# Rows of the split activations at other byte offsets, a halved opening that ends with the second tile alone, and column sums placed between products

## The reference, cut to what matters

```python
def swiglu(h, w1, w2):
    a, b = jnp.split(h @ w1, 2, axis=-1)
    return (jax.nn.silu(a) * b) @ w2

h = h + 0.5 * ml[2] * swiglu(modulate(h, norm_g[l, 0], ml[0], ml[1]), ffn_w1[l, 0], ffn_w2[l, 0])   # FFN, D_FF = 2816
...
y_l, y_c = ab_mixer(...)   # layer 0: input projection, retention heads and an S5 scan with a GLU, output projection
y_l, y_c = na_mixer(...)   # layer 1: k, q, v projections, neighbourhood attention, output projection
...
h = h + 0.5 * ml[8] * swiglu(modulate(h, norm_g[l, 2], ml[6], ml[7]), ffn_w1[l, 1], ffn_w2[l, 1])
```

## Time and profile before

| | |
|---|---|
| median of three runs | 1868.72 us (1867.93 to 1872.14) |
| the profiled execution, its own time | 1870.24 us |
| its span | 1868.4 us |
| TensorE busy | 1795.8 us (96%) |
| TensorE's weight loads | 1529.7 us (82%) |
| DVE busy | 1194.8 us (64%) |
| ACT busy | 726.6 us (39%) |
| POOL busy | 61.9 us (3%) |
| mean granted TensorE clock | 0.982 of 2.4 GHz |
| chain that ended last | TensorE 84%, DVE 8%, ACT 5%, issue 2%, DMA 1% |
| read from HBM | 255.79 MB, 137 GB/s over the span |

### The profile page before, as it was taken

How to read it: one execution, slowest core, us unless ns; L and a number is a source line. 1 busy time by engine, 2 the same in 40 slices (tenths; PEclk the granted TensorE clock), 3 DMA queues, 4 the chain that set the end, 5 groups by cost and what they waited for, 6 DMA issues and landing times.

```text
span 1868.4 us, 25748 instructions
## 1 busy us (share of the span) xinstructions
PE 1795.8 (96%) x9970; PEld 1529.7 (82%) x9970; DVE 1194.8 (64%) x1890; ACT 726.6 (39%) x1027; POOL 61.9 (3%) x41
## 2 busy tenths in 40 slices
PE   7999999998988899999999999999999999989998
PEld 5788888887787588888888888888888898689997
DVE  4677677777999745776677367766333434855554
ACT  4422222336888734231222242212222333744343
POOL 0000000020000010000000200000002000010001
PEclk8999999999999899999999999999999999989999
DMA  8454455331110123544553335444213342034543
GB/s 328 182 204 156 169 193 194 113 125 60 54 35 35 46 90 113 210 161 154 196 208 125 115 136 194 154 158 175 106 65 115 124 169 68 2 136 174 186 171 122
DMA packets 40440, 257.81 MB, mean 138 GB/s; under 512 B 4752, under 2 KB 6032, under 8 KB 15536
## 3 DMA queue, kind: packets, MB, share of 16 engines
q1 hardware_dynamic: 40368, 256.86, 38.0%
HBM read 255.79 MB, written 1.05 MB: 137 GB/s over the span
## 4 chain that ended last, share of the span: by engine, by line
PE 84%; DVE 8%; ACT 5%; issue 2%; DMA 1%; POOL 0%; DVEq 0%; SPq 0%; ACTq 0%; POOLq 0%
PE ps_all L1797 26%; PE ps_all L1801 25%; PE ps_all L1798 25%; DVE w_lo L1047 2%; ACT w_hi L565 2%; PE ps_all L1793 1%; PE banks L2355 1%; DVE sq_acc L1527 1%; PE banks L2169 1%; PE ps_all L2332 0%; PE banks L1949 0%; DVE normed L1536 0%; PE banks L2332 0%; PE ps_all L1987 0%; DVE scaled L1518 0%
## 5 line engine op out<-in xcount | busy, mean ns | idle before, releaser
L1797 PE MATMUL ps_all<-a_hi,w_lo 128*128 128x512 f32 (+1 forms) x1832 | 655.1, 358 | 17.4 <-DVE w_lo L1047 8.6
L1801 PE MATMUL ps_all<-a_lo,w_hi 128*128 128x512 f32 (+1 forms) x1832 | 650.1, 355 | 0.1
L1798 PE MATMUL ps_all<-a_hi,w_hi 128*128 128x512 f32 (+1 forms) x1832 | 650.1, 355 | 0.0
L1047 DVE TENSOR_TENSOR w_lo<-w_raw,w_hi 128x2048 fp32r<-128x2048 f32 (+2 forms) x179 | 365.2, 2040 | 161.2 <-ACT w_hi L565 161.0
L565 ACT ACTIVATE w_hi<-w_raw 128x2048 fp32r<-128x2048 f32 (+2 forms) x179 | 306.0, 1709 | 332.7 <-PE ps_all L1801 316.2
L1797 PEld LDWEIGHTS ps_all<-a_hi,w_lo 128*128 128x128 f32 x1832 | 348.9, 190 | 69.1 <-DVE w_lo L1047 10.7
L1801 PEld LDWEIGHTS ps_all<-a_lo,w_hi 128*128 128x128 f32 x1832 | 348.9, 190 | 48.4 <-DVE a_lo L1201 0.3
L1798 PEld LDWEIGHTS ps_all<-a_hi,w_hi 128*128 128x128 f32 x1832 | 348.9, 190 | 47.1 <-issue 0.2
L1059 DVE SCALAR_TENSOR_TENSOR mod_junk<-mod_raw,cond 128x1024 bf16<-128x1024 f32 x256 | 302.8, 1221 | 7.4 <-ACT cond L593 5.4
L1797 PE MATMUL ps_all<-g_hi,w_lo 128*128 128x512 f32 (+1 forms) x734 | 264.4, 360 | 2.1 <-DVE w_lo L1047 2.1
L1801 PE MATMUL ps_all<-g_lo,w_hi 128*128 128x512 f32 (+1 forms) x734 | 263.3, 359 | 0.0
(11 more groups left out here) (280 smaller groups left out, 1528.6 us busy)
## 6 DMA issues: line engine op xcount, KB each, us to landing
w_raw<-in_tiles SPq DMA_DIRECT2D x118, 1024.0 KB, 4.8
mod_raw<-in_w_mod SPq DMA_DIRECT2D x64, 1024.0 KB, 4.8
w_raw<-in_tiles SPq DMA_DIRECT2D x32, 768.0 KB, 4.1
w_raw<-in_tiles SPq DMA_DIRECT2D x32, 640.0 KB, 3.8
start_w<-in_w_start SPq DMA_DIRECT2D x8, 1024.0 KB, 19.9
bias<-in_na_bias SPq DMA_DIRECT2D x2, 1536.0 KB, 9.0
h<-in_h SPq DMA_DIRECT2D x4, 512.0 KB, 5.7
cond<-in_cond SPq DMA_DIRECT2D x2, 1024.0 KB, 18.2
```

The costliest lines, as they stand in the source:

```text
L1047: nc.vector.tensor_tensor(w_lo[:, slot, 0:size], w_raw[:, slot, 0:size], w_hi[:, slot, 0:size].bitcast(F32), ALU.subtract).then_inc(lo_rea ...
L1797: pe.matmul(dst, w[1], x[0], start=start, stop=False)
L1798: pe.matmul(dst, w[0], x[0], start=False, stop=False)
L1801: return pe.matmul(dst, w[0], x[1], start=False, stop=stop_)
```

## The change

- A tensor `rows_gap` of 64 bytes a partition is declared behind `kint`, ahead of `g_hi` and of all that lies over the FFN's tensors: each of them starts 64 bytes later. `g` rows of 512 tokens then start at 1088 of 2048, their latent halves (closings) at 64.
- `LAST_AT` = columns 112 to 367 of a row, in place of 256 to 511, holds the 256 latent tokens of na_out's input (`a`) and of ffn3's `a` and `g` rows. The former start at 1024 of 2048, the latter at 1536. PSUM, `gated` and `h` keep their places.
- `halved_opening`: its last eight units are (0, 4..7), then (1, 4..7), in place of a mixed order that ended (0, 7), (1, 6), (1, 7). `opening`: (0, 7) is followed by six units of slot 1, not four, and (0, 2) comes before (1, 0).
- `mixer0`: ret_in's first weights are split before `us` is copied from tile 0 (ACT), and ahead of DVE's last of the eight copies.
- `close`: the column sums of the latent half, and those of the second-last square, are put between products of the latent half; `part(range(1), 1)` and the like say which products.

```diff
@@ -229,6 +229,7 @@
...
         kint = sbuf("kint", [P, 32], mybir.dt.int32)
+        sbuf("rows_gap", [P, 16])
 
@@ -340,6 +341,8 @@
...
         FFN_T0 = (0, 0, 0, NCTX)
+        LAST_AT = slice(112, 112 + NLAT)
+        FFN_AT = [slice(t0, T) for t0 in FFN_T0[:3]] + [LAST_AT]
 
@@ -575,7 +578,7 @@
...
                     act.wait_ge(ps_free[slot], BASE[segment] // 2 + it + 1)
-                    g = g_hi[:, bass.ds(2 * it + slot, 1), t0:T].rearrange("p a t -> p (a t)")
+                    g = g_hi[:, bass.ds(2 * it + slot, 1), FFN_AT[int(segment[3])]].rearrange("p a t -> p (a t)")
                     nc.scalar.activation(g, gated[:, slot, t0:T], ACT.Copy).then_inc(g_hi_ready, 1)
@@ -710,10 +713,8 @@
...
                     act.wait_ge(scaled_ready, KT * PART_BASE[k_norm] + k + 1)
-                    for half, b, e in halves(t0):
-                        ins = nc.scalar.activation(a_hi[:, k, b:e], ahead[k % 4][:, b:e], ACT.Identity,
-                                                   bias=modv[:, col(k_norm, 0) + k, half:half + 1])
-                    ins.then_inc(a_hi_ready, 1)
+                    nc.scalar.activation(a_hi[:, k, LAST_AT], ahead[k % 4][:, NCTX:T], ACT.Identity,
+                                         bias=modv[:, col(k_norm, 0) + k, 1:2]).then_inc(a_hi_ready, 1)
 
@@ -779,8 +780,8 @@
...
                 for j in range(2):
-                    if j:
-                        split_hi(BASE["s5_in"] + j + 1, 2048, 1 - j)
+                    if j == 0:
+                        split_hi(BASE["ret_in"], 2048, 0)
                     act.wait_ge(pe_done, BASE["s5_in"] + j + 1)
@@ -1003,7 +1004,7 @@
...
                     nc.scalar.activation(
-                        a_hi[:, tile, NCTX:T].rearrange("p (r c) -> p r c", c=GRID_W),
+                        a_hi[:, tile, LAST_AT].rearrange("p (r c) -> p r c", c=GRID_W),
                         bank[tile % 2][:, 0:NLAT].rearrange("p (r c) -> p r c", c=GRID_W)[:, :, ::-1],
@@ -1088,7 +1089,7 @@
...
                     dve.wait_ge(g_hi_ready, g_base(segment) + j + 1)
-                    hi, lo = [x[:, bass.ds(j, 1), t0:T].rearrange("p a t -> p (a t)") for x in (g_hi, g_lo)]
+                    hi, lo = [x[:, bass.ds(j, 1), FFN_AT[int(segment[3])]].rearrange("p a t -> p (a t)") for x in (g_hi, g_lo)]
                     nc.vector.tensor_tensor(lo, gated[:, slot, t0:T], hi.bitcast(F32), ALU.subtract).then_inc(g_split, 1)
@@ -1265,11 +1266,9 @@
...
                     dve.wait_ge(a_hi_ready, KT * PART_BASE[k_norm] + k + 1)
-                    for half, b, e in halves(t0):
-                        ins = nc.vector.scalar_tensor_tensor(a_lo[:, k, b:e], ahead[k % 4][:, b:e],
-                                                             modv[:, col(k_norm, 0) + k, half:half + 1],
-                                                             a_hi[:, k, b:e].bitcast(F32), ALU.add, ALU.subtract)
-                    ins.then_inc(a_ready, 1)
+                    nc.vector.scalar_tensor_tensor(a_lo[:, k, LAST_AT], ahead[k % 4][:, NCTX:T],
+                                                   modv[:, col(k_norm, 0) + k, 1:2],
+                                                   a_hi[:, k, LAST_AT].bitcast(F32), ALU.add, ALU.subtract).then_inc(a_ready, 1)
                     if k < KT - 2:
@@ -1458,12 +1457,12 @@
...
                 for j in range(2):
-                    if j:
-                        split_lo(BASE["s5_in"] + j + 1, 2048, 1 - j)
                     dve.wait_ge(pe_done, BASE["s5_in"] + j + 1)
...
                             if q == 3 and s == 3:
+                                if j == 0:
+                                    split_lo(BASE["ret_in"], 2048, 0)
                                 dve.wait_ge(S["us_act"], j + 1)
@@ -1707,9 +1706,9 @@
...
                     nc.vector.tensor_tensor(
-                        a_lo[:, tile, NCTX:T].rearrange("p (r c) -> p r c", c=GRID_W),
+                        a_lo[:, tile, LAST_AT].rearrange("p (r c) -> p r c", c=GRID_W),
                         bank[tile % 2][:, 0:NLAT].rearrange("p (r c) -> p r c", c=GRID_W)[:, :, ::-1],
-                        a_hi[:, tile, NCTX:T].bitcast(F32).rearrange("p (r c) -> p r c", c=GRID_W),
+                        a_hi[:, tile, LAST_AT].bitcast(F32).rearrange("p (r c) -> p r c", c=GRID_W),
                         ALU.subtract).then_inc(N["mix"], 1)
@@ -1811,7 +1810,8 @@
...
                                 mm = three(ps[slot][:, m, t0:T], [x[:, k, m] for x in w],
-                                           (a_hi[:, k, t0:T], a_lo[:, k, t0:T]), k == 0, k == KT - 1)
+                                           (a_hi[:, k, FFN_AT[int(segment[3])]], a_lo[:, k, FFN_AT[int(segment[3])]]),
+                                           k == 0, k == KT - 1)
                         mm.then_inc(pe_done, 1)
@@ -1836,7 +1836,7 @@
...
                         mm = three(ps[slot][:, 0, t0:T], [x[:, k] for x in w],
-                                   (g_hi[:, k, t0:T], g_lo[:, k, t0:T]), k == 0, k == K - 1)
+                                   (g_hi[:, k, FFN_AT[f]], g_lo[:, k, FFN_AT[f]]), k == 0, k == K - 1)
                     mm.then_inc(pe_done, 1)
@@ -1867,20 +1867,23 @@
...
                 half_sums(sq_acc, 0, 0)
-                half_sums(sq_acc, 0, 1)
+                part(range(1), 1)
                 if first == KT - 1:
...
                     half_sums(sq[:, 0], 1, 0)
-                    half_sums(sq[:, 0], 1, 1).then_inc(sq_summed, 1)
-                else:
-                    part(range(1), 1)
+                    part(range(1, 2), 1)
                 pe.wait_ge(sq_part, LAST_SQUARES[k_norm])
...
                 mm.then_inc(half_summed, 1)
-                part(range(0 if first == KT - 1 else 1, 4), 1)
+                part(range(2 if first == KT - 1 else 1, 4), 1)
+                half_sums(sq_acc, 0, 1)
+                part(range(4, 5), 1)
+                if first == KT - 1:
+                    half_sums(sq[:, 0], 1, 1).then_inc(sq_summed, 1)
+                part(range(5, 6), 1)
                 spread_half(k_norm, 0)
-                part(range(4, K), 1).then_inc(pe_done, 1)
+                part(range(6, K), 1).then_inc(pe_done, 1)
 
@@ -1930,7 +1933,7 @@
...
                         unit(slot, k, NCTX, T, 1)
-                for slot, k in ((0, 4), (0, 5), (1, 4), (0, 6), (1, 5), (0, 7), (1, 6), (1, 7)):
+                for slot, k in ((0, 4), (0, 5), (0, 6), (0, 7), (1, 4), (1, 5), (1, 6), (1, 7)):
                     if (slot, k) == (1, 4):
@@ -2025,10 +2028,10 @@
...
 
-                segment, t0 = AFTER_NORM[k_norm], FFN_T0[int(AFTER_NORM[k_norm][3])] if "ffn" in AFTER_NORM[k_norm] else 0
+                segment, t0 = AFTER_NORM[k_norm], NCTX
                 n = BASE[segment]
-                order = [(0, 0), (0, 1), (1, 0), (0, 2), (1, 1), (0, 3), (1, 2), (0, 4), (1, 3), (0, 5), (0, 6), (0, 7),
-                         (1, 4), (1, 5), (1, 6), (1, 7)]
+                order = [(0, 0), (0, 1), (0, 2), (1, 0), (0, 3), (1, 1), (0, 4), (0, 5), (0, 6), (0, 7),
+                         (1, 2), (1, 3), (1, 4), (1, 5), (1, 6), (1, 7)]
                 for slot, k in order:
@@ -2040,7 +2043,7 @@
...
                         mm = three(ps[slot][:, m, t0:T], [x[:, k, m] for x in w],
-                                   (a_hi[:, k, t0:T], a_lo[:, k, t0:T]), k == 0, k == KT - 1, lo)
+                                   (a_hi[:, k, LAST_AT], a_lo[:, k, LAST_AT]), k == 0, k == KT - 1, lo)
                     if k == KT - 1:
@@ -2282,7 +2285,7 @@
...
 
-            def pair_tile(segment, j, K, at, before=None, t0=0, lat=False):
+            def pair_tile(segment, j, K, at, before=None, t0=0, rows=None):
 
@@ -2293,7 +2296,8 @@
...
                         mm = three(ps[slot][:, m, t0:T], [x[:, k, m] for x in w],
-                                   (a_hi[:, at + k, t0:T], a_lo[:, at + k, t0:T]), k == 0, k == K - 1)
+                                   (a_hi[:, at + k, rows or slice(t0, T)], a_lo[:, at + k, rows or slice(t0, T)]),
+                                   k == 0, k == K - 1)
                 mm.then_inc(pe_done, 1)
@@ -2368,7 +2372,7 @@
...
                 for j in range(4):
-                    pair_tile("na_out", j, 8, 0, lambda k: pe.wait_ge(N["mix"], k + 1) if j == 0 else None, NCTX)
+                    pair_tile("na_out", j, 8, 0, lambda k: pe.wait_ge(N["mix"], k + 1) if j == 0 else None, NCTX, LAST_AT)
 
```

## The result

The changed kernel takes 1839.19 us (median of four runs, 1838.46 to 1840.89) against 1870.23 for the kernel before (median of four); the ratio is 0.983, 95% interval 0.9819 to 0.9842. That is 31.0 us faster; 1836 was forecast. Timed once more beside two other kernels, it took 1839.03 against 1870.73. Of the 3.2 us between forecast and result, 1.5 are from the time of the kernel before: 1836 was counted from the median of three runs, 1868.72, and the fourth made it 1870.23. The profiled execution has 1839.42 us, a span of 1837.6 and a mean granted clock of 0.987 (before: 1870.24, 1868.4 and 0.982).

What follows compares the result with a forecast made beforehand. Outside the mixers TensorE's step between products and its idle times bound the kernel. Rows 10.0 - 0.8 + 1.3 + 2.9, openings 7.6 + 4.1 + 1.9, clock 1.7 + 1.7 + 1.4, sums 1.3: 33.1 off 1868.72, 1836 us; range 1828 to 1850.

Steps and rivals of the forecast that it cites:

- Part 1: Rows moved by bytes: 512-column products from `g` fall from 233.3 to 226.7 ns, 10.0 us; further terms -0.8, +1.3, +2.9.
- the 0.8: Loss in the three closings, whose 180 products from `g` go to the bad start: 1.2 us, partly hidden under DVE's work.
- the bound of 3.5: Loss in us if ffn3's 528 narrow `g` products, moved to byte 1536, ran slower there; no change was taken.
- The ring in ffn3: End of tile, Silu, gating, g_hi, w_hi, w_lo, tile j+2 limits the up pass: half of 0.32 per tile kept, 2.9 us.
- The rival of 7.0 us: ffn3's weights ring gives way and its up pass keeps all of 7.0 us: 1832; chance 0.05.
- Part 2: Openings end with the second tile alone, removing or shortening TensorE's idle times: 7.6 (ffn1, ffn2, na_k) + 4.1 (s5_in) + 1.9 (ffn3).
- a sign named for being wrong: Idle times turning up within tile 0 of an opening, before L1801, for `a_lo`, would show the prediction wrong.
- The clock: Half-clock stretches behind idle times at s5_in, ffn2 and ffn3 vanish with the idle times: 1.7 + 1.7 + 1.4 us.
- rival 2: Clock still falls in closings and after short idle times that stay: 9.1 us less gain, 1845; chance 0.12.
- the retention stage shifts as a whole: ret_in's rows, evacuation and scan start from s5_in's resumed product, so the first mixer keeps its gain of 4.1 us.
- waits for POOL before and after: 0: First mixer's closing (ab_out) waits for POOL either way, so moving its column sums changes nothing: 0.
- Part 3: Column sums between products keep the clock up in three closings; the openings give back 0.45 each, 1.3 us.

Runs made afterwards that it cites:

- orders alone: The changed kernel without the 64-byte gap and with `LAST_AT` back at the old columns, so only the new opening, copy and column-sum orders; 1854.66 us, ratio 0.9906.
- rows alone: The kernel before with only the 64-byte gap, `LAST_AT` and its uses, orders as they were; 1856.62 us, ratio 0.992.
- v3: The changed kernel with both the edit of v1 and the edit of v2; 1832.09 us, ratio 0.9789.
- v1: The changed kernel, but in ffn3 w_hi and w_lo of tile j+2 are made ahead of g_hi and g_lo of tile j; 1834.14 us, ratio 0.981.
- Old sums: The changed kernel with `close` as it was before, column sums back in their old places; 1840.47 us, ratio 0.9837.
- v2: The changed kernel with 1/rms spread ahead of the second-last square's latent sums in FFN closings, two rows earlier in the first mixer's; 1835.96 us, ratio 0.9815.
- v4: v3 with the `a` rows of na_out and ffn3 back at byte 64 of 512, `g` rows left at 1536; 1837.82 us.

## Why the prediction was right, point by point

The forecast was 33.1 us, and the two traces differ by 30.8. By stretch, the terms of the sum put where they belong, and measured:

| | forecast | measured |
|---|---|---|
| three down0 (3 x 288 x 6.67 ns) | 5.8 | 5.7 |
| ffn0's closing to ffn1.up0 | 9.8 | 6.9 |
| ffn1.down1 to ffn2.up0 | 5.7 | 6.0 |
| ffn2.down1, second mixer, ffn3.up0 | 10.4 | 10.4 |
| ffn3.up1 | 1.5 | 1.4 |
| start, ffn3's down passes and end | 0 | 0.3 |

(The up1 passes of ffn0 to ffn2 give the 0.1 that is left.)

- *Part 1, `g` at 64.* Right: 226.7 ns in all 498 triples; the tiles of the down1 passes give 1.39 between *orders alone* and after, 210 x 6.67 ns. The closings' products did go to 120, but the 0.8 does not show: the closings of *orders alone* are not shorter by it. In the first half of a closing 30 products cost 0.2 more, but behind it TensorE waits for the last square (a step of 0.50 in *orders alone*, of 0.32 after, both in ffn1's closing), which takes it up. ffn3's `g` rows at 1536 behave as at 1024: the bound of 3.5 did not come in. The ground given, start modulo 512, was too coarse: the period is 256.
- *na_out.* Its 192 products took 23.01 us before and 21.77 after, 1.24 against 1.3. In *rows alone* and in v3 they took 22.6, at 117.8.
- *The ring in ffn3.* Right: 10 tiles of up1 came 0.14 nearer, forecast 0.15. That the weights' ring bound them is what v1 and v3 show together: with it away no wait is left in the pass. The rival of 7.0 us needs more than the ring: with the ring away a pass gave 0.5 in v1 and 2.6 in v3, by the step that TensorE happened to take.
- *Part 2.* Idle times are gone at ffn1, ffn2 and na_k, and 0.56 and 0.65 are left at s5_in and ffn3, forecast 0.6. ret_in's first tile starts 6.93 earlier where s5_in's second ended 2.79 earlier: 4.14 of 4.1. ffn3's (0, 2) waits 0.85 for `a_lo`, not 0.2. With this and the 0.20 and 0.60 in the other openings, a sign named for being wrong came true in small: idle times for `a_lo` inside an opening.
- *The clock.* Six stretches at half clock gone, as forecast; rival 2 did not happen in the FFNs. *Old sums* shows the price of a fall in a closing: 1.54.
- *The step that failed* is that the first mixer keeps all: "the retention stage shifts as a whole", and for its closing "waits for POOL before and after: 0". 2.9 us are missing there. Up to 0.3 more than forecast was gained before (7.67 by the product at 440.80, counted from the start of ffn0.down1, which itself comes 0.77 earlier; 7.4 was forecast); 3.2 were then lost in three places. First, with the clock up the product that stood at 440.80 comes 8.44 earlier, but `qk` (ACT's timeline, before and after) only 7.57: ACT had waited 2.19 for TensorE there and now works without a pause from the second tile's copies on. 0.9 lost.

```profile
450.21 1.02 ACT L798 ACTIVATE qk<-ps_all 128x1024 f32<-128x1024 f32 x1 [2.19 <-PE ps_all L1801]
```

```profile
442.64 1.02 ACT L799 ACTIVATE qk<-ps_all 128x1024 f32<-128x1024 f32 x1
```

  Second, the mixer's closing spread 1.4 later, and ffn1's opening waits 0.60 for `a_lo`: the closing's first sum comes 5.83 earlier than before and ffn1.down0 7.62 earlier, so closing and opening gave 1.8 of the 2.4 forecast; 0.6 lost. v2 won 0.8 back. Third, the extra stretch at 633.4 took 1.7: up to it DVE's rows are 7.6 earlier than before, behind it 5.9. It is in both traces of the changed kernel, in *orders alone*, *old sums*, v1 and v4, but not in v2 and v3, whose mixer has the same code there; neither the kernel before nor *rows alone* has it. What makes it come is open.
- *Part 3.* 1.3 forecast. Its terms were right in kind, but one was left out. Where a fall is spared, 1.54 - 0.9 = 0.6 is left, near the 0.45 of the forecast; where there would have been none, 0.9 is lost, and that had been put at 0. With falls in six of nine closings that makes 0.1 a closing (my estimate), 0.4 in place of 1.3. v2 has the gain without the cost in the FFN closings. Half w_lo is still last before product (1, 0), as forecast; at ffn2's opening it ends at 1075.04, and the product starts at 1075.10 (DVE's and TensorE's timeline):

```profile
1073.82 1.22 DVE L1226 TENSOR_TENSOR w_lo<-w_raw,w_hi 128x1024 fp32r<-128x1024 f32 x1
```

```profile
1075.10 0.39 PE L1796 MATMUL ps_all<-a_hi,w_lo 128*128 128x256 f32 x1
```

## What to carry to other kernels

Before moving work about, measure the distance of starts of like products from each source: a fixed surplus that follows the byte where a row starts can be won by a gap between tensors, here one of 64 bytes. When a closing is rearranged to keep TensorE's clock up, put what the next stage waits for (the spreading) ahead of the sums that nobody waits for, and count rows in products, since a row is six in one closing and twelve in another. And when a wait is removed, check what the engine then does: in v1 it went on at a slower step of its own, in v3 at the faster one.

## What the runs showed of the hardware

- The step of float32 products depends on the start of the moving rows modulo 256 bytes: with 512 columns 226.7 to 227.4 ns at 64, 229 to 230 at 128, 232 to 235 at the eight other offsets tried; with 256 columns 113.3 at 0 and 120.0 at 64.
- With 256 columns from start 0, TensorE takes one of two steps, 113.3 or 117.8 ns, and keeps it until its next wait (at the bound of a tile): in the changed kernel's ffn3.up1 runs of 94 and of 46 products between waits are wholly at one or the other, in v1 all 508 at 117.8, and in v3 all 508 at 113.3. *Orders alone* has 117.8 in ffn3.down0 (34.99 us) where the kernel before, with the same rows, has 113.3 (34.04). From start 64 there was no such choice, always 120.0. What decides is open; it makes the same pass of v1 and v3, with the same code, differ by 2.1 us.
- Half clock came in six of nine FFN closings with the one-column sums together and in none of 21 with products between: the same instructions in another order. In the first mixer's closing that order did not keep it away (three of eight traces).
